# Gate and up weights of the last twenty experts in runs of 32 KB per partition, 4 MB to a transfer

## What is computed

```python
def expert_ffn(xb, e, w_gate_up, b_gate_up, w_down, b_down):
    gu = xb @ w_gate_up[e] + b_gate_up[e]          # (1024 x 2048) per expert: 8 MiB
    gate = jnp.minimum(gu[:, :D_FF], SWIGLU_LIMIT)
    up = jnp.clip(gu[:, D_FF:], -SWIGLU_LIMIT, SWIGLU_LIMIT)
    h = (up + 1.0) * gate * jax.nn.sigmoid(SWIGLU_ALPHA * gate)
    return h @ w_down[e] + b_down[e]               # (1024 x 1024) per expert: 4 MiB
```

## Time and profile before

| | us |
|---|---|
| median of 3 runs | 1027.58 (1027.56 to 1031.42) |
| span of the profiled execution, first to last instruction | 1026.2 |
| what lies around the span, median less span | 1.4 |
| TensorE busy | 978.7 (95%) |
| VectorE, ScalarE busy | 215.3, 104.8 |
| moved by DMA | 418.5 MB in 35392 packets, 408 GB/s over the span |

### The profile page before, as it was taken

The page is one execution under the profiler, slowest core; times in us unless marked ns, Lnnn a source line. Parts: engine busy times, 40 slices in busy tenths (PEclk is TensorE's granted clock), DMA queues, the critical chain, the costliest instruction groups (busy, mean ns, idle before and its releaser), DMA issues.

```text
span 1026.2 us, 11169 instructions
## 1 busy us (share of the span) xinstructions
PE 978.7 (95%) x4610; PEld 418.4 (41%) x4610; DVE 215.3 (21%) x472; ACT 104.8 (10%) x181; POOL 8.5 (1%) x27
## 2 busy tenths in 40 slices
PE   9999999999999999899999999999999989898996
PEld 7685534343434333333434343433334333332432
DVE  2234423121121211121212112121112121120121
ACT  2251200000000000000000000000000000000102
POOL 0010000000000000000000000000000000000000
PEclk9999999999999999999999999999999999999999
DMA  9967799999999999999999999999999999999995
GB/s 337 420 274 291 266 383 427 429 428 429 428 429 429 429 429 427 428 427 426 429 429 429 429 429 429 427 429 429 428 428 429 428 427 429 429 429 427 427 426 215
DMA packets 35392, 418.51 MB, mean 408 GB/s; under 512 B 4364, under 2 KB 5032, under 8 KB 10152
## 3 DMA queue, kind: packets, MB, share of 16 engines
q1 hardware_dynamic: 33584, 417.09, 96.7%
q10 hardware_dynamic: 1784, 1.08, 0.4%
HBM read 417.10 MB, written 1.05 MB: 407 GB/s over the span
## 4 chain that ended last, share of the span: by engine, by line
PE 69%; DMA 25%; DVE 3%; issue 2%; ACT 1%; SPq 0%; DVEq 0%; ACTq 0%
PE bank L1349 56%; DMA ring<-in_w_gate_up_dram 13%; PE acc L1349 12%; DMA ring<-in_w_down_dram 12%; DVE area L1160 1%; DVE area L1157 1%; PE bank L1751 1%; DVE area L1096 1%; DMA ring<-in_w_in_dram 1%; ACT wpool L745 1%; DVE sel L858 0%; DVE area L1164 0%; ACT late L819 0%; PE bank L1582 0%; DVE masks L1073 0%
## 5 line engine op out<-in xcount | busy, mean ns | idle before, releaser
L1349 PE MATMUL bank<-ring,area 128*64 128x512 f32 (+1 forms) x1832 | 411.5, 594 | 13.4 <-DMA ring<-in_w_gate_up_dram 13.4
L1349 PEld LDWEIGHTS bank<-ring,area 128*64 128x64 f32 (+1 forms) x1832 | 132.1, 138 | 283.9 <-issue 254.1
L1349 PE MATMUL bank<-ring,wpool 128*64 128x512 f32 x864 | 192.3, 596 | 11.4 <-DMA ring<-in_w_down_dram 6.6
L1154 DVE TENSOR_SCALAR area<-bank 128x512 f32<-128x512 f32 x31 | 21.4, 692 | 444.2 <-PE bank L1349 444.2
L1349 PEld LDWEIGHTS bank<-ring,wpool 128*64 128x64 f32 x864 | 59.8, 137 | 123.9 <-issue 107.9
L741 ACT ACTIVATE bank<-area 128x512 f32<-128x512 f32 x32 | 19.2, 602 | 495.2 <-DVE area L1154 495.2
L1349 PE MATMUL bank<-masks,xres 128*128 128x128 f32 x492 | 66.0, 287 | 2.1 <-DVE masks L1073 0.3
L1349 PEld LDWEIGHTS bank<-masks,xres 128*128 128x128 f32 x492 | 60.4, 196 | 17.7 <-issue 16.6
L1178 DVE COPY wide<-bank 64x512 f32<-64x512 f32 x30 | 20.8, 694 | 198.9 <-PE bank L1349 192.6
L1349 PE MATMUL acc<-wide,masks 128*128 128x512 f32 x120 | 55.5, 606 | 0.0
L1349 PE MATMUL bank<-area 128*64 128x512 f32 (+2 forms) x228 | 47.0, 559 | 0.6 <-DVE area L931 0.5
(11 more groups left out here) (195 smaller groups left out, 429.1 us busy)
## 6 DMA issues: line engine op xcount, KB each, us to landing
ring<-in_w_gate_up_dram SPq DMA_DIRECT2D x113, 2048.0 KB, 24.5
ring<-in_w_down_dram SPq DMA_DIRECT2D x54, 2048.0 KB, 25.6
area<-in_w_gate_up_dram SPq DMA_DIRECT2D x13, 2048.0 KB, 18.9
late<-in_w_down_dram SPq DMA_DIRECT2D x5, 2048.0 KB, 17.2
ring<-in_w_down_dram SPq DMA_DIRECT2D x6, 1024.0 KB, 41.9
ring<-in_w_in_dram SPq DMA_DIRECT2D x8, 512.0 KB, 9.9
ring<-in_w_in_dram SPq DMA_DIRECT2D x4, 1024.0 KB, 17.1
ring<-in_w_out_dram SPq DMA_DIRECT2D x4, 1024.0 KB, 15.7
```

The lines of the kernel that those rows point to most:

```text
L1154: v.tensor_scalar(gatec, gbank[:], LIMIT, None, ALU.min).then_inc(gc, 1)
L1349: return t.matmul(o, l, r, start=start, stop=stop, skip_group_check=True)
```

## The change

The rows go four to a partition instead of two (`rows_of`, and with it `d_step`, `g2rows`, `turn_g2`, `wrouter`). That holds for all 32 experts. In the ring stage, experts 12 to 31, four chunks of gate/up are loaded by one transfer (`load_four`, 4 MiB, 32 KB in one run for each partition) into four neighbouring places, once all four are free, and one semaphore covers the four. Experts 0 to 11 keep transfers of two chunks: each partition's 16 KB run is now one half of a 32 KB group, and the other half comes with the next transfer. Down weights are loaded as before. The places of the ring stage are permuted so that the fours are neighbours, `ring_loads` issues in another order, and in the router two of the transposes move behind a later wait.

```diff
@@ -77,7 +77,9 @@
     SHARED, LAST = 5, 11
     PAIR_PLACES = (FRONT + BACK + LATE)[0::2] + [(FRONT + BACK)[2 * SHARED]]
-    ROUND = [PAIR_PLACES[p] for p in (0, 1, 2, 3, 4, 8, 9, LAST)]
+    ROUND_OF = (0, 1, 2, 3, 8, 9, 4, LAST)
+    ROUND = [PAIR_PLACES[p] for p in ROUND_OF]
+    QUAD = 4
     assert len(FIRST_PLACES) == PER_PAIR and sorted(ROUND) == list(range(0, RING, 2))
     assert PER_BODY % RING == 0 and UP_CHUNKS == 8 and DOWN_CHUNKS == 4 and (NE - FIRST) % BODY == 0
@@ -123,12 +125,29 @@
...
-    LAST_LOADS = [(0, c, 24 + c) for c in range(0, 8, 2)]
-    LAST_LOADS += [(1, c, 32 + c if c < 4 else None) for c in range(0, 8, 2)]
+    LAST_LOADS = [(0, c, 24 + c) for c in (0, QUAD)] + [(1, 0, 32), (1, QUAD, None)]
     LAST_LOADS += [(r, 8 + c, 36 + 4 * r + c) for r in range(2) for c in (0, 2)]
@@ -192,7 +211,7 @@
         diag = [gatec[:, tt * P:(tt + 1) * P] for tt in range(TT)]
-        g2rows = part(7744, 2 * P)[0:4, :]
+        g2rows = part(7744, 4 * P)[0:2, :]
         wide = sb("wide", [P, D])
@@ -267,8 +286,8 @@
         G2 = vecT[:, 16:24]
         def d_step(src, k):
-            lo = (k // 2) * 2 * P
-            return src[:, lo + k % 2:lo + 2 * P:2]
+            lo = (k // 4) * 4 * P
+            return src[:, lo + k % 4:lo + 4 * P:4]
         BG, BU, BY, BM = bank[4], bank[5], bank[6], bank[7]
@@ -336,6 +355,11 @@
                 return part((slot - RING + 1) * CHUNK, 2 * CHUNK)
             return ring[:, slot * CHUNK:(slot + 2) * CHUNK]
+        def quad_place(slot):
+            if slot >= RING:
+                return part(CHUNK, QUAD * CHUNK)
+            return ring[:, slot * CHUNK:(slot + QUAD) * CHUNK]
         def place(slot):
             return pair_place(slot & ~1)[:, (slot % 2) * CHUNK:(slot % 2 + 1) * CHUNK]
@@ -362,8 +386,8 @@
         def rows_of(e, c, n):
             if c < UP_CHUNKS:
-                src = rows["wgu"][bass.ds(e * D + (c // 2) * 2 * P, 2 * P), :]
-                return src.rearrange("(p s) f -> p s f", s=2)[:, c % 2:c % 2 + n, :]
+                src = rows["wgu"][bass.ds(e * D + (c // 4) * 4 * P, 4 * P), :]
+                return src.rearrange("(p s) f -> p s f", s=4)[:, c % 4:c % 4 + n, :]
             c -= UP_CHUNKS
             src = rows["wd"][bass.ds(e * F + (c // 2) * 4 * P, 4 * P), :]
             return src.rearrange("(p s) f -> p s f", s=4)[:, 2 * (c % 2):2 * (c % 2) + 2 * n, :]
@@ -474,22 +498,33 @@
                     else:
                         load_pair(e + 2, p)
+            def load_four(e, c, s):
+                dst = quad_place(s).rearrange("p (s f) -> p s f", s=QUAD)
+                sp.dma_start(dst, rows_of(e, c, QUAD)).then_inc(chunk_in[s // 2], 16)
             def ring_loads():
                 e = FIRST - 2
-                for j, place_of in enumerate(ROUND):
-                    p = LAST if j == len(ROUND) - 1 else PAIR_PLACES.index(place_of)
-                    if p > SHARED and j == SHARED:
+                for j, p in enumerate(ROUND_OF):
+                    if j == 4:
                         sp.wait_ge(chunks_used, e * PER_EXPERT + 2 * SHARED + 2)
                         load_pair(e, LAST)
                     sp.wait_ge(chunks_used, e * PER_EXPERT + 2 * p + 2)
-                    load_two(FIRST + j // 6, j % 6 * 2, place_of)
+                    r, c = FIRST + j // 6, j % 6 * 2
+                    if c >= UP_CHUNKS:
+                        load_two(r, c, ROUND[j])
+                    elif c % QUAD:
+                        load_four(r, c - 2, ROUND[j - 1])
             def load_expert(e, m0, begun=0):
-                for c in range(begun, PER_EXPERT, 2):
-                    sp.wait_ge(chunks_used, e * PER_EXPERT + (c + 1) - (RING - 1))
+                for c in range(begun, UP_CHUNKS, QUAD):
+                    sp.wait_ge(chunks_used, e * PER_EXPERT + (c + QUAD) - RING)
+                    load_four(e, c, slot_of(m0 + c))
+                for c in range(UP_CHUNKS, PER_EXPERT, 2):
+                    sp.wait_ge(chunks_used, e * PER_EXPERT + (c + 2) - RING)
                     load_two(e, c, slot_of(m0 + c))
             first_loads()
@@ -509,7 +544,10 @@
             for r, c, m in LAST_LOADS:
                 if m is None:
-                    load_two(base // PER_EXPERT + 2 + r, c, RING + c - 4)
+                    load_four(base // PER_EXPERT + 2 + r, c, RING)
+                elif c < UP_CHUNKS:
+                    sp.wait_ge(chunks_used, base + m + QUAD - RING)
+                    load_four(base // PER_EXPERT + 2 + r, c, slot_of(m))
                 elif m < LAST_SINGLE:
                     sp.wait_ge(chunks_used, base + m + 2 - RING)
                     load_two(base // PER_EXPERT + 2 + r, c, slot_of(m))
@@ -586,7 +624,7 @@
                                               (pool_scale, 12, 4))):
                 v = src[0, :, :] if len(src.shape) == 3 else src.rearrange("l (r c) -> (l r) c", c=P)
                 act.dma_start(vecs[lo:lo + n, :], v).then_inc(vecs_in[i], 16)
-            act.dma_start(g2rows, norm2_g.rearrange("l (r c) -> (l r) c", c=2 * P)).then_inc(vecs_in[3], 16)
+            act.dma_start(g2rows, norm2_g.rearrange("l (r c) -> (l r) c", c=4 * P)).then_inc(vecs_in[3], 16)
             act.wait_ge(edge_c, 3)
             a.activation(stat[:, 15:16], epsc[:], ACT.Sqrt).then_inc(warm, 1)
@@ -607,8 +645,8 @@
                              bias=epsc[:]).then_inc(rtd, 1)
             act.dma_start(wpool[:], w_pool[0].rearrange("g c d -> c g d")).then_inc(wpool_in, 16)
-            act.dma_start(wrouter[:].rearrange("p (c s) e -> p c s e", s=2), w_router[0].rearrange(
-                "(c p s) e -> p c s e", p=P, s=2)).then_inc(
+            act.dma_start(wrouter[:].rearrange("p (c s) e -> p c s e", s=4), w_router[0].rearrange(
+                "(c p s) e -> p c s e", p=P, s=4)).then_inc(
                 wrouter_in, 16)
             act.dma_start(brow[:], b_router.broadcast_to([P, NE])).then_inc(brow_in, 16)
             act.dma_start(fg, final_norm_g.rearrange("(r c) -> r c", c=P)).then_inc(fg_in, 16)
@@ -1368,8 +1406,8 @@
                 pe.wait_ge(vecs_in[3], 16)
-                for s in range(2):
-                    m = t.transpose(bank[4][:, s:8:2], g2rows[:, s::2], ident[0:4, 0:4])
+                for s in range(4):
+                    m = t.transpose(bank[4][:, s:8:4], g2rows[:, s::4], ident[0:2, 0:2])
                 m.then_inc(vec_t, 1)
             def turn(src, tt, halves=(0, 1), stepped=True):
@@ -1599,11 +1637,10 @@
             turn_last(6, 0, 4)
             output(4, 6, 1)
             output(4, 7, 1).then_inc(wo_ok, 1)
-            pe.wait_ge(x2_ok, 4)
-            turn_last(4, 4, 2)
             pe.wait_ge(tr_a, 9)
             logits((0, 1))
             pe.wait_ge(x2_ok, 5)
+            turn_last(4, 4, 2)
             turn_last(5, 6, 2)
             logits((2, 3))
             pe.wait_ge(tr_c, 3)
@@ -1684,24 +1721,37 @@
...
+                    pair = ring_pair(m)
+                    pe.wait_ge(chunk_in[pair], i * (16 * ring_signals(pair)) + 16 * loads_of(m, stage))
...
```

More of the change, by code:

```diff
@@ L125, in loads_of, with ring_signal, ring_signals, ring_pair @@
                     + (PAIR_PLACES[SINGLE_LOAD] // 2 == pair))
-        return signals(pair) + n // RING + 1
-    LAST_LOADS = [(0, c, 24 + c) for c in range(0, 8, 2)]
-    LAST_LOADS += [(1, c, 32 + c if c < 4 else None) for c in range(0, 8, 2)]
+        pair = ring_pair(n)
+        return signals(pair) + sum(ring_signal(m) == pair for m in range(0, n + 1, 2))
+    def ring_signal(m):
+        slot = slot_of(m)
+        c = m % PER_EXPERT
+        if c < UP_CHUNKS:
+            return slot // QUAD * 2 if c % QUAD == 0 else None
+        return slot // 2
+    def ring_signals(pair):
+        return sum(ring_signal(m) == pair for m in range(0, PER_BODY, 2))
+    def ring_pair(m):
+        return slot_of(m) // QUAD * 2 if m % PER_EXPERT < UP_CHUNKS else slot_of(m) // 2
+    LAST_LOADS = [(0, c, 24 + c) for c in (0, QUAD)] + [(1, 0, 32), (1, QUAD, None)]
     LAST_LOADS += [(r, 8 + c, 36 + 4 * r + c) for r in range(2) for c in (0, 2)]
@@ L1686, in chunk_wait, with last_signals @@
                     pe.wait_ge(chunk_in[slot // 2], 16 * loads_of(m, stage))
-                else:
-                    between = 16 * (pair_signals(slot // 2) if stage == "pair" else PER_BODY // RING)
-                    pe.wait_ge(chunk_in[slot // 2], i * between + 16 * loads_of(m, stage))
-                return slot
-            ring_at = {(r, c + n): m if m is None else m + n for r, c, m in LAST_LOADS for n in range(2)}
+                elif stage == "pair":
+                    pe.wait_ge(chunk_in[slot // 2],
+                               i * (16 * pair_signals(slot // 2)) + 16 * loads_of(m, stage))
+                else:
+                    pair = ring_pair(m)
+                    pe.wait_ge(chunk_in[pair], i * (16 * ring_signals(pair)) + 16 * loads_of(m, stage))
+                return slot
```

(14 more changed lines are left out.)

## The result

Before 1027.66 us (1027.56 to 1031.42, 4 runs), after 1053.8 us (1053.02 to 1054.43, 4 runs): ratio 1.0245, 95% interval 1.0231 to 1.0259. The profiled execution's span is 1051.1 us, 24.9 above that of before. The forecast was 1027.2, in a range from 1023.0 to 1031.5.

A forecast was written before the change was run, and what follows sets the result against it. DMA was taken to bound the kernel from about 150 us, plus a tail. 1026.2 - 2.4 + 1.5 + 0 + 0.5 + 0 = 1025.8 us of span, plus 1.4 to the runs' median, gave 1027.2 us, range 1023.0 to 1031.5.

The forecast's parts named there:

- part 4: Other order of rows: gathers reading with a step of four words cost nothing; with its other terms +0.5 us.
- Rival B: Steady expert loop: TensorE falls behind the fours, beyond 1.2 us more per expert; 1045 us if the clock halves; chance 0.08.
- Part 1: Gate/up loads of 20 experts: 32 KB runs go as one packet each, fewer packets save 2.4 us.
- Part 2: TensorE waits for four chunks at once: free in the steady part, +1.5 us in the tail, experts 30 and 31.
- Part 3: SP issues later, needing four free places: 6.4 chunks stay queued, no gap, 0 us; ends 0 and +3.6.
- Part 4's other terms: More transposes in `turn_g2`, +0.33 us, and moved router transposes, +0.15; together +0.5 us, ends 0 and 0.8.
- Part 5: Experts 0 to 11: loading gate/up in half groups costs 0, with 3.5 us to either side.
- A: Weight loads: longer runs raise the rate itself to 436 GB/s, giving 1022.9 us; chance 0.12.
- C: Experts 0 to 11: half groups are read less well; 1034 us at 3%, 1030.7 at 1.5%; chance 0.14.
- D: Gate/up transfers: the 32 KB run is cut, packets stay at 16 KB, only costs remain, 1029.6 us; chance 0.16.

The follow-up runs named there:

- e10: Kernel before, with the second half of each looped gather reading the residual at a step of four words; 1033.91 us, ratio 1.005.
- e1: Changed kernel, with only the gathers reading the residual at a step of two words as before; 1028.69 us, ratio 1.0007 to before.
- e6: Changed kernel with the residual kept in the weights' order and gate/up of experts 30 and 31 in two-chunk transfers; 1027.08 us, ratio 0.9996 to before.
- e7: Changed kernel with gathers at a step of two words and gate/up of experts 30 and 31 in two-chunk transfers; 1028.0 us, ratio 1.0 to before.
- e11: Changed kernel with the residual in the weights' order, fours for experts 12 to 27, two-chunk transfers for 28 to 31; 1025.91 us, ratio 0.9981 to before.
- e12: Changed kernel with the residual in the weights' order and every gate/up transfer of two chunks, no fours; 1027.99 us, ratio 1.0 to before.
- e5: Changed kernel, whole computation, with the residual kept in the weights' order so gathers read neighbouring words; 1027.57 us, ratio 0.9996 to before.
- e2: Kernel before, with only the gathers reading the residual at a step of four words; 1053.9 us, ratio 1.0254.
- e8: Kernel before, with the four transposes of the hidden rows made plain matmuls against the identity; 1046.43 us.

## Why the prediction was wrong, step by step

**The step that failed** is in part 4: "So nothing", for `d_step` with a step of four words. I took a price from a row with the same step but of another instruction, the transposes, and let it outweigh the rule of the Trainium skill (page "SBUF — State Buffer", section "Specifications (TRN2)") that spoke against the change, without making that a rival with a chance of its own; the nearest row wasn't the same operation, and I gave no upper bound. At half the rate for both halves of a gather, an estimate, it was 2 x 2.05 us more per pair, and from the earlier trace rows TensorE's own pair would have been up to 58.9 us, over the transfers' 58.7: a rival at once. Measured: 328 ns a weight load instead of 196, +1.85 us per 16 records, 57.6 us per pair, +26.1 us in all. Rival B had the right consequence, TensorE falling behind, but looked for it in the steady part (1.2 us to spare per expert). The backlog decides sooner: e10 loses 5.8 us with a pair's own work at 56.6. B's pause does come in kernels with fours whose TensorE isn't late, and the clock did fall behind one or two of them (e1, e6, e7, e11), at 1.6 to 1.7 us each, not 7.1; in the kernel after there is no such pause.

**Part 1 held.** 32 KB runs go as one packet: 29372 packets, where 29632 were forecast (5120 large and 640 small fewer, as said; I had not counted the queue of the router weights and gains, 260 fewer). 428 to 431 GB/s, e12 against e11, is 0.7%; on the 391.5 us of these loads 2.7 us, by my terms 2.4.

**Part 2 held in size, with a flaw in its place.** From e5 to e11, fours to the end or not, the ratio to before goes from 0.9996 to 0.9981, 1.5 us, which was my price (the intervals touch). But it is not paid in the last two experts alone (e6 gave nothing back): the late start on expert 29's four is carried on.

**Part 3 was wrong: there is a gap.** The slice at 450 us moves 234 GB/s. Most of that comes with the slower gathers (e2, without fours, has 286), and the fours deepen it; where TensorE bounds the end it costs nothing. But without the slow gathers the fours leave a gap of their own: in that slice e1 moves 410 and e5 404 GB/s, where before and e12, without fours, move 427. That is 1.0 and 1.4 us of transfers, inside the ends I gave, and by these rates it takes back a part of what the longer runs give. From e1, 450 to 455:

```profile
450.00:455.00 5.00, 5.00 (x24) 1.48 (x22) 1.12 (x2) 0.59 (x1) 0.00 (x0) 1.00 0.89 334
```

**Part 4's other terms** were 0.5 us: in e1, whose first gather begins at 118.57 where it was 117.69, they come to 0.9. **Part 5 held**: 428 GB/s with half groups (e12); the 403 and 401 GB/s of the kernel after in slices 7 and 8 come with the slower gathers, as in e2 (399 in slice 7). Rivals A, C and D are out: 430 to 431 GB/s over the stretch with fours and not 436, no loss by half groups, no cut.

**The signs of being wrong.** All three that I named came: slices over 2% off, a gap of DMA, and the granted clock, which left 1.00 between 978 and 984 us. The clock isn't the cause: e2 and e1 settle that, and the gather that fell into it took 3.74 us for 16 records (983.68 - 979.94), no more than the others.

## What to carry to other kernels

A layout that suits the transfers can cost the readers more: before a DMA run is lengthened, list every operand whose step changes, and price each by a row of the same instruction at that step, or, if there is none, by double its time. Keep the 128 columns that one load takes at most two words apart, or regroup the tensor once (four copies here) and read neighbours. And where an engine works off a backlog, its spare time is what it waits for data over the whole run, not its pace against the bound: here 20 us over 15 pairs, so that 1.0 us more per pair cost under 2 us in all, 1.85 cost 5.8, and 2.85, with the first pair's gathers slower too, cost 26.

## What the runs showed that I had not expected

- A step of four words makes a float32 matmul's weight load take 330 ns instead of 196, and its streamed operand pays too; a transpose's load takes 209 to 212 ns at a step of two or four, and 141 with none.
- With a step of four the weight load doesn't go by TensorE's clock. In the kernel after the granted clock was 0.50 of the full 2.4 GHz, thus 1.2 GHz, from 980 to 982 us, and the loads there took 330 ns as at full clock; in e8, at 0.53 from 625.1 to 628.6, loads with a step of two took 331 ns instead of 196. The kernel after, then e8:

```profile
980.00:982.00 2.00, 2.00 (x10) 2.00 (x10) 0.00 (x0) 0.60 (x1) 0.00 (x0) 0.50 1.10 475
...
L1387 PEld LDWEIGHTS bank<-masks,xres x16: 330/330/333, 979.7 to 983.2; 128*128 128x128 f32 x16
```
```profile
625.10:628.60 3.50, 3.50 (x19) 3.28 (x20) 0.00 (x0) 0.60 (x1) 0.00 (x0) 0.53 1.00 426
...
L1349 PEld LDWEIGHTS bank<-masks,xres x16: 196/331/336, 625.0 to 627.9; 128*128 128x128 f32 x16
```

- TensorE's clock falls now and then, and the length of the pause before it doesn't decide it alone. In e1, behind a pause of 2.52 us, 32 records took 8.78 us instead of 7.09, at 0.62 on average, thus partly at 1.2 GHz; a pause of 2.34 us in the same trace left it at 1.00. In e7 it fell behind one pause of 2.18 us and not behind another. In the kernel after it fell with no pause over 0.42 us anywhere near. What sets it off is open. In e1 it cost 1.7 us, ahead of the tail, where nothing hides it:

```profile
420.59 3.65 PE L1391 MATMUL bank<-ring,wpool 128*64 128x512 f32 x16 [2.34 <-DMA ring<-in_w_down_dram]
...
943.66 8.78 PE L1391 MATMUL bank<-ring,area 128*64 128x512 f32 x32 [2.52 <-DMA ring<-in_w_gate_up_dram]
```
```profile
943.66:948.00 4.34, 4.34 (x14) 1.37 (x16) 0.00 (x0) 0.00 (x0) 0.00 (x0) 0.62 1.01 430
```
